# Hybrid encoder layer with grouped experts: one word per block from the table, rows turned before the product, lists in two parts, addition ahead of gather

## What is computed

```
def _moe(h, router_w, router_bias, w_gate, w_up, w_down):
    expert, gates = _route(hf, router_w, router_bias)      # 32 experts, two per token
    ...
    def expert_block(args):
        xb, e = args
        return (jax.nn.silu(xb @ w_gate[e]) * (xb @ w_up[e])) @ w_down[e]
    ...
    out = jnp.zeros((t, d), h.dtype).at[buf_tok].add(
        yb.reshape(rows, d) * buf_g[:, None].astype(h.dtype))

x = _layer_norm(ALPHA * x + (1.0 + g2) * y, ln_ffn_g[l], ln_ffn_b[l])
```

## Time and profile before

| | us |
|---|---|
| median of 3 runs | 1923.19 |
| lowest, highest | 1918.34, 1924.17 |
| the profiled execution | 1921.33 |
| its span, first to last instruction | 1919.5 |
| up to the first block's matmuls | 893.95 |
| blocks, until x1 is read again | 893.95 to 1866.26 |
| reading, last norm, store | 1866.26 to the end |

### The profile page before, as it was taken

One profiled execution on the slowest core, in us unless ns is written; L12 is line 12 of the kernel. 1 busy time (PEld: TensorE's weight loads), 2 busy tenths in 40 slices (PEclk: granted clock), 3 DMA queues, 4 the chain that ended last, 5 costly groups with the idle time before them and its releaser, 6 DMA issues. The chain is left out here.

```text
span 1919.5 us, 55830 instructions
## 1 busy us (share of the span) xinstructions
PE 1541.8 (80%) x17568; PEld 999.4 (52%) x17569; DVE 1015.9 (53%) x2033; ACT 712.8 (37%) x1398; POOL 548.3 (29%) x704
## 2 busy tenths in 40 slices
PE   3999879985899999943887888878888887888840
PEld 2777558863676666632444444444444444444420
DVE  5578778973578888872333332333333334333328
ACT  2313462236576666512323221232222234331217
POOL 0000010000001111122444444444544544544443
PEclk9999889996899999966999999999999999999975
DMA  7657674229433333258879753788567699873247
GB/s 300 220 198 268 204 251 143 88 66 341 167 111 111 120 112 113 97 206 298 320 233 353 248 172 70 272 308 293 172 191 244 220 373 400 282 265 87 38 93 319
DMA packets 130625, 401.51 MB, mean 209 GB/s; under 512 B 15183, under 2 KB 69839, under 8 KB 101760
## 3 DMA queue, kind: packets, MB, share of 16 engines
q1 hardware_dynamic: 95936, 343.85, 47.4%
q0 software_dynamic: 33616, 55.63, 13.3%
q10 hardware_dynamic: 1008, 1.22, 0.2%
HBM read 327.71 MB, written 75.04 MB: 210 GB/s over the span
## 5 line engine op out<-in xcount | busy, mean ns | idle before, releaser
L2034 PE MATMUL psum_gate_up<-gate_up_now,xT 128*32 128x256 f32 x9088 | 535.9, 389 | 172.6 <-DVE xT L2244 169.0
L2034 PEld LDWEIGHTS psum_gate_up<-gate_up_now,xT 128*32 128x32 f32 x9088 | 297.0, 112 | 411.2 <-issue 165.9
L1974 POOL DMA_INDIRECT x_kept<-y_rows,add_index x144 | 230.9, 1603 | 394.6 <-DVE y_rows L2262 387.7
L2047 PE MATMUL psum_y<-down_now,hT 128*32 128x256 f32 x4544 | 274.0, 381 | 5.2 <-issue 3.2
L2087 ACT ACTIVATE gate_silu<-psum_gate_up 128x128 f32<-128x128 f32 x142 | 39.1, 275 | 479.0 <-PE psum_gate_up L2034 479.0
L2047 PEld LDWEIGHTS psum_y<-down_now,hT 128*32 128x32 f32 x4544 | 150.2, 110 | 107.8 <-issue 20.2
L520 PE MATMUL proj_bank<-x_hi,w_hi 128*128 128x512 f32 x448 | 182.4, 407 | 19.8 <-DVE w_lo L632 8.8
L2250 DVE TENSOR_TENSOR hidden<-gate_silu,psum_gate_up 128x128 f32<-128x128 f32 x142 | 40.4, 285 | 298.2 <-ACT gate_silu L2087 236.8
L1959 POOL DMA_INDIRECT x_rows<-h_kept,row_index x148 | 156.5, 1057 | 116.2 <-POOL row_index L1949 102.4
L521 PE MATMUL proj_bank<-x_lo,w_hi 128*128 128x512 f32 x448 | 177.3, 396 | 0.0
L522 PE MATMUL proj_bank<-x_hi,w_lo 128*128 128x512 f32 x448 | 177.1, 395 | 0.0
(11 more groups left out here) (278 smaller groups left out, 2179.2 us busy)
## 6 DMA issues: line engine op xcount, KB each, us to landing
gate_up_raw<-in_w_gate_up SPq DMA_DIRECT2D x128, 1024.0 KB
down_raw<-in_w_down SPq DMA_DIRECT2D x64, 1024.0 KB
x_raw<-in_ada_w SPq DMA_DIRECT2D x16, 1024.0 KB, 4.8
w_raw<-in_w_in SPq DMA_DIRECT2D x28, 512.0 KB
x_raw<-in_xT SPq DMA_DIRECT2D x16, 512.0 KB, 9.7
q_kept<-q_stage SPq DMA_DIRECT2D x32, 256.0 KB, 2.8
q_tile<-q_kept SPq DMA_DIRECT2D x16, 512.0 KB, 4.2
wo<-w_out_kept SPq DMA_DIRECT2D x8, 1024.0 KB, 13.5
```

Source lines behind the costliest of these rows:

```text
L1974: pool.indirect_dma_start(io["x1_rows"], bass.IndirectOffsetOnAxis(add_index[i][:, 0:1], 0), y_rows[:, i, :], None, compute_op=ALU.add).th ...
L2034: last = mm(quarter_of(GU, q)[:, 0:QUARTER], xT[:, k, :], gu_now[:, k, q * QUARTER:(q + 1) * QUARTER], start=(k == 0), stop=(k == DC - 1))
L2047: last = mm(quarter_of(Y, q)[:, 0:QUARTER], hT[:, c, :], down_now[:, c, q * QUARTER:(q + 1) * QUARTER], start=(c == 0), stop=(c == EC - 1))
```

## The change

- **Table.** Three values a block instead of six. One is a word that packs what was four: whether the next block starts an expert, whether this one does, the gate-and-up slot and the expert. The down slot is the expert's lowest bit. ScalarE and VectorE load the word once per block. PE loads nothing in its loop: its waits count by block, and ScalarE and VectorE raise those counters also in blocks without copies.
- **Rows early.** ScalarE keeps x of block j+1 ahead of the weight copies and silu of block j, VectorE turns it ahead of `hide`.
- **Weights freed.** SyncE waits for one count per expert, raised in the expert's first block, instead of the single copies.
- **Row weight.** The gate of each row is copied by GpSimd to `row_weights`, VectorE reads it there and needs no column.
- **Lists.** The column order is by list position, then expert, so the first 256 columns hold every expert's first eight blocks. They are loaded and prepared first, the other 1792 later. Block 0's x and table come ahead of most of the first weight copies on ScalarE.
- **GpSimd.** Addition of block j first, then the gather of block j+4. The last round has no gathers. ScalarE, not GpSimd, waits for the additions of real blocks and frees the rereading of x1.

```
-TABLE_ROWS = 6
-EXPERT, COLUMN, IS_FIRST, N_ALL, GU_SLOT, DOWN_SLOT = range(TABLE_ROWS)
+TABLE_ROWS = 3
+WORD, COLUMN, N_ALL = range(TABLE_ROWS)
+WORD_MAX = 16 * E - 1
 LIST_COLS = E * SLOTS
+EARLY_COLS = 8 * E
...
-                stt(addr[:, :, :], n_before[:, :, :], float(1 - ROWS * LIST_COLS), row[:, :, :], ALU.mult, ALU.add
+                stt(addr[:, :, :], n_before[:, :, :], float(E - ROWS * LIST_COLS), row[:, :, :], ALU.mult, ALU.add
...
+        def parts_of(word):
+
+
+            next_first, first = word & 1, (word >> 1) & 1
+            return next_first, first, word >> 4, ((word >> 2) & 3).with_bounds(min_val=0, max_val=GU_SLOTS - 1)
...
-            for q in range(QUARTERS):
-                sp.dma_start(quarter_of(lists, q)[:, 1:LIST_COLS, :].rearrange("p a b -> p (a b)"),
-                             io["list_rows"][:, 2:2 * LIST_COLS]).then_inc(lists_landed, 16)
+            for landed, first, last in ((early_landed, 1, EARLY_COLS), (lists_landed, EARLY_COLS, LIST_COLS)):
+                for q in range(QUARTERS):
+                    sp.dma_start(quarter_of(lists, q)[:, first:last, :].rearrange("p a b -> p (a b)"),
+                                 io["list_rows"][:, 2 * first:2 * last]).then_inc(landed, 16)
...
-                        last = PIECE * (piece + 1)
-                        sp.wait_ge(gu_by_act, len(GU_BY_ACT) * (e - GU_SLOTS) + sum(k < last for k in GU_BY_ACT))
-                        sp.wait_ge(gu_by_dve, len(GU_BY_DVE) * (e - GU_SLOTS) + sum(k < last for k in GU_BY_DVE))
+                        sp.wait_ge(gu_freed, e - GU_SLOTS + 1)
...
+                ps.tensor_copy(weights[:, i:i + 1], entry_of(column, 1).bitcast(F32)).then_inc(weights_ready, 1)
...
-            def round_of(turn):
+            def round_of(turn, with_next=True):
                 for i in range(RING):
-                    gather(RING * turn + RING + i, i)
                     add_rows(RING * turn + i, i, turn)
+                    if with_next:
+                        gather(RING * turn + RING + i, i)
...
+            last_round = (blocks(pool, but=RING) + (RING - 1)) // RING
             for i in range(1, RING):
                 gather(i, i)
+            pool.wait_ge(quartered, 1)
             round_of(0)
-            with pool.Fori(1, n_rounds) as turn:
+            with pool.Fori(1, last_round) as turn:
                 round_of(turn)
+            round_of(last_round, with_next=False)
             for i in range(RING):
-                wait_apart(pool, (table_ready, 2), (y_added[i], 16 * n_rounds))
-                wait_apart(pool, (table_ready, 2), (x_gathered[i], 16 * n_rounds + 16))
-            pool.sem_inc(all_added, 1)
...
-            def gate_up(j, e):
+            def gate_up(j):
                 pe.wait_ge(x_turned, j + 1)
                 if not isinstance(j, int) or j > 0:
                     pe.wait_ge(hidden_ready, j)
                 for k in range(DC):
                     if k in GU_BY_ACT:
-                        pe.wait_ge(gu_by_act, len(GU_BY_ACT) * e + (GU_BY_ACT.index(k) + 1))
+                        pe.wait_ge(gu_by_act, len(GU_BY_ACT) * j + (GU_BY_ACT.index(k) + 1))
                     else:
-                        pe.wait_ge(gu_by_dve, len(GU_BY_DVE) * e + (GU_BY_DVE.index(k) + 1))
+                        pe.wait_ge(gu_by_dve, len(GU_BY_DVE) * j + (GU_BY_DVE.index(k) + 1))
...
-                following = table_value(pe, EXPERT, j, 0, E - 1)
-                before = table_value(pe, EXPERT, j - 1, 0, E - 1)
-                gate_up(j, following)
-                down(j - 1, before)
-            down(n - 1, E - 1)
+                gate_up(j)
+                down(j - 1)
+            down(n - 1)
...
-            def next_block(j):
-                next_first = table_value(act, IS_FIRST, j + 1, 0, 1)
-                expert, slot = (table_value(act, EXPERT, j + 1, 0, E - 1),
-                                table_value(act, GU_SLOT, j + 1, 0, GU_SLOTS - 1))
-                with act.If(next_first > 0):
-                    copy_gate_up(expert, slot, j, GU_BY_ACT[:-1])
-                silu(j)
+            def step(j):
+                next_first, first, expert, slot = parts_of(table_value(act, WORD, j, 0, WORD_MAX))
                 keep_x(j + 1)
                 with act.If(next_first > 0):
-                    copy_gate_up(expert, slot, j, GU_BY_ACT[-1:])
+                    copy_gate_up(expert + 1, slot, j, GU_BY_ACT[:-1])
+                silu(j)
+                with act.If(next_first > 0):
+                    copy_gate_up(expert + 1, slot, j, GU_BY_ACT[-1:])
+                with act.Else():
+                    act.sem_inc(gu_by_act, len(GU_BY_ACT))
+                if isinstance(j, int) and j == 0:
+                    act.sem_inc(gu_freed, 1)
+                else:
+                    with act.If(first > 0):
+                        act.sem_inc(gu_freed, 1)
+                        copy_down(expert, expert & 1, j - 1)
...
+            copy_gate_up(0, 0, None, GU_BY_ACT[:2])
+            act.wait_ge(early_landed, 16 * QUARTERS)
+            af(lists[:, 1:EARLY_COLS, 0], lists[:, 1:EARLY_COLS, 0], ACT.Identity, bias=C["quarter"]
+               ).then_inc(early_quartered, 1)
             act.wait_ge(counted, 3)
-            nc.scalar.copy(table[:, 4:6, :], B[2][0:1, :].rearrange("p (a b) -> p a b", a=2)[:, :, 0:NJ]
+            nc.scalar.copy(table[:, COLUMN:N_ALL + 1, :], B[2][0:1, :].rearrange("p (a b) -> p a b", a=2)[:, :, 0:NJ]
                            ).then_inc(table_ready, 1)
-            act.wait_ge(lists_landed, 16 * QUARTERS)
-            af(lists[:, 1:LIST_COLS, 0], lists[:, 1:LIST_COLS, 0], ACT.Identity, bias=C["quarter"]
-               ).then_inc(quartered, 1)
             keep_x(0)
+            copy_gate_up(0, 0, None, GU_BY_ACT[2:])
...
+                act.wait_ge(y_added[i], (n + (RING - 1 - i)) // RING * 16)
+            act.sem_inc(all_added, 1)
...
             def weigh_rows(j):
-                column = table_value(dve, COLUMN, j, 0, LIST_COLS + RING - 1)
                 dve.wait_ge(down_chunk_done, EC * (j + 1))
+                dve.wait_ge(weights_ready, j + 1)
                 dve.wait_ge(y_room, j + 1)
-                stt(in_ring(y_rows, j), Y[:, 0:QUARTER], entry_of(column, 1).bitcast(F32), gain2[:, :],
+                stt(in_ring(y_rows, j), Y[:, 0:QUARTER], weights[:, bass.ds(j % RING, 1)], gain2[:, :],
                     ALU.mult, ALU.mult).then_inc(y_ready, 1)
 
-            def next_block(j):
-                next_first = table_value(dve, IS_FIRST, j + 1, 0, 1)
-                expert, slot = (table_value(dve, EXPERT, j + 1, 0, E - 1),
-                                table_value(dve, GU_SLOT, j + 1, 0, GU_SLOTS - 1))
+            def free_down(e):
+                dve.wait_ge(down_by_act, len(DOWN_BY_ACT) * (e + 1))
+                dve.wait_ge(down_by_dve, len(DOWN_BY_DVE) * (e + 1))
+                dve.sem_inc(down_freed, 1)
+
+            def step(j):
+                next_first, first, expert, slot = parts_of(table_value(dve, WORD, j, 0, WORD_MAX))
                 with dve.If(next_first > 0):
-                    copy_gate_up(expert, slot, j)
+                    copy_gate_up(expert + 1, slot, j)
+                turn_x(j + 1)
                 hide(j)
-                turn_x(j + 1)
+                with dve.If(next_first < 1):
+                    dve.sem_inc(gu_by_dve, len(GU_BY_DVE))
+                if not isinstance(j, int) or j > 0:
+                    with dve.If(first > 0):
+                        copy_down(expert, expert & 1, j - 1)
+                        free_down(expert)
+                turn_hidden(j)
+                if not isinstance(j, int) or j > 0:
+                    weigh_rows(j - 1)
```

More of the change, by code:

```diff
@@ L1502, in place @@
                    places.unsqueeze(3).to_broadcast([P, 2, 2, n_starts]), ALU.is_le).then_inc(pos_steps, pos_n.one())
-                ts(row[:, :, :], experts, float(SLOTS), None, ALU.mult).then_inc(pos_steps, pos_n.one())
                 dve.wait_ge(pos_steps, pos_n.now())
@@ L2274, in _ @@
             copy_gate_up(0, 0, None)
             dve.wait_ge(counted, 3)
-            for i in range(2):
-                last = copy(table[:, 2 * i:2 * i + 2, :],
-                            B[i][0:1, :].rearrange("p (a b) -> p a b", a=2)[:, :, 0:NJ])
-            last.then_inc(table_ready, 1)
+            copy(table[:, WORD, 0:P], B[0][0:1, 0:P])
+            copy(table[:, WORD, P:NJ], B[1][0:1, 0:NJ - P]).then_inc(table_ready, 1)
             turn_x(0)
             copy_down(0, 0, None)
+            free_down(0)
```

117 lines of the change are left out of this document (54 added, 63 removed).

## The result

| | before | after |
|---|---|---|
| median of 4 runs each, us | 1921.68 | **1960.93** |
| lowest, highest | 1918.34, 1924.17 | 1957.61, 1961.89 |
| span of the profiled execution | 1919.5 | 1958.7 |

The changed kernel is slower: ratio 1.020 (95% interval 1.018 to 1.022). The forecast was 1824 us, faster.

A forecast was written before the change was run, and what follows sets the result against it. Ordinary blocks were taken as bound by PE's sequencer, blocks around expert changes by VectorE. 190 - 5 - 98 - 10 = 77, + 9 + 13 = 99 us saved: 1822 profiled, 1824 us as median; range 1765 to 1892.

The forecast's parts named there:

- Part 1: PE's loop: both table loads go, so blocks run at 5.3 us, 740 for the stage, 190 us saved.
- rival C: PE's loop: the jump costs what the loads seemed to (1.1 us), ordinary blocks stay at 6.3; 1901 us, chance 0.08.
- Part 2: GpSimd's order: gathers issued behind the addition start one block later; give back 98 us (28 to 170).
- The gather under load: Gather's time with DMA busy: 5.5 us, between 4.9 (behind one weight piece) and 6.9 (one row); alone 2.3.
- The slack of ordinary blocks: Gather's lead in ordinary blocks: 5.05 us where it was about 12; 6 us given back for late weightings.
- Rival D: Gathers last over about 8.2 us when busy, additions ahead in their queue; at 8.5 slower, 1942 us, chance 0.05.
- Rival A: Gathers in the expert stage are never late (2.3 us each): 1754 us, chance 0.15.
- Rival B: GpSimd becomes the bound, making the row weight too: cycle 5.17, or 5.93 us with a dearer hand-over; 1887, chance 0.12.
- Part 3: Weight loading: raw weights freed only at the expert's first block; give back 10 us (0 to 30).
- Part 4: Start: only 255 list columns awaited, block 0 at about 885.9, 8 us sooner; gain 9 us (5 to 11).
- Part 5: End: dead blocks' gathers and additions go, ScalarE waits for real additions only, 4.2 us; gain 13 us (9 to 14).

The follow-up runs named there:

- the best kernel: Changed kernel with row weight, then gather, ahead of the addition, rings of five blocks instead of four, and raw gate-up weights freed once copied: 1726.33 us, ratio 0.898.

## Why the prediction was wrong, point by point

**Part 1, PE's loop: right.** The pace is 5.18, not 5.3: the jump costs nothing that a row shows, and rival C is out. That is 17 us better than counted. The idle time of 0.88 behind a finished xT is gone.

**Part 2, GpSimd's order: the step that failed**, by two terms and a missing third.

- *The gather under load.* I took 5.5 us, from one piece plus 2.3, against the one row that showed 6.9. It is 7.66 on average and up to 8.64. The row had told it, and the start of a stage was no outlier: in that same trace 68 gathers landed 5.3 to 7.8 us after their start, which no wait showed, since the x copies came 3.7 us or more behind the landings.
- *The slack of ordinary blocks.* With 5.5 against 5.05 I gave ordinary blocks 6 us. With 7.66 they are late too: 117 us. At the changes the number was right (17 busy, I had 20), the price was not: 7.4 us each instead of 4.1, and 1.9 at the quiet ones instead of 0.9. For the quiet ones I had read 2.3 us from when the bytes stopped; until ScalarE's copy starts it is 3.2.
- *What lateness does to PE.* I priced the waits alone. Behind an idle time of 3.36 us the 64 matmuls of 1878.21 took 6.46 instead of 3.64, at a granted clock of 0.54:

```profile
1878.21 6.46 PE L2047 MATMUL psum_gate_up<-gate_up_now,xT 128*32 128x256 f32 x64 [3.36 <-DVE hidden L2264]
```

Over the stage PE is busy 798.10 us at 0.92 for what the best kernel does in 730.32 at 1.00: of the 262 us, 187 are PE's waits and 74 are matmuls slower than 5.18 a block, 68 of them more than there. I had no term for that.

**Sum.** For the stage I had 740 + 113 = 853 us; it is 724 + 262 = 985. The failing terms are 149 of give-back, less 17 of better pace.

**Rival D had the direction, at a chance of 0.05, but not its condition.** It put the turning point at 8.2 us and the time at 8.5 at 1942. The mean stayed below 8.2 and the kernel was slower all the same; D had no term for the slower matmuls (74 us) nor for GpSimd's lag (14 us by its own run). D's reason, that gathers last so long because additions stand ahead of them, was wrong in the main: additions make 1.1 us of the 7.66, and the longer ring gives 0.943 with the addition still ahead. What the order costs is the lead, one block. **Rival A** would not have come out even with quiet gathers: 1840 and, with GpSimd's lag gone, 1790, not 1754. **Rival B** is real but smaller, 5.45 instead of 5.93, hidden in the changed kernel and the next thing to bound it once gathers are in time.

**Part 3** 7.7 for 10, measured on the kernel with the row weight ahead of the gather. **Part 4.** Block 0 starts at 888.45, not 885.9, as its own gather took 8.3 us (879.21 to 887.52); the third block is 7.8 sooner, for 9:

```profile
879.21 1.02 POOL L1962 DMA_INDIRECT x_rows<-h_kept,row_index  x1 [0.27 <-POOL row_index L1952]
...
887.52 0.41 ACT L2102 COPY x_now<-x_rows 128x256 f32<-128x256 f32 x1 [3.55 <-DMA x_rows<-h_kept,row_index]
...
888.45 6.41 PE L2047 MATMUL psum_gate_up<-gate_up_now,xT 128*32 128x256 f32 x64 [4.95 <-DVE xT L2258]
```

**Part 5.** From the down product of block 140 to the first load of x1 it is 1904.27 - 1889.67 = 14.6 for 23.66: 9.1 gained, not 13. The last addition to the load is 4.2 as I had it. The last down product came late, waiting 3.28 for a weighting that itself waited for its row weight, and ran at a low clock:

```profile
1889.67 1.90 PE L2056 MATMUL psum_y<-down_now,hT 128*32 128x256 f32 x32
...
1894.85 3.26 PE L2056 MATMUL psum_y<-down_now,hT 128*32 128x256 f32 x32 [3.28 <-DVE y_rows L2276]
...
1900.10 1.58 POOL L1978 DMA_INDIRECT x_kept<-y_rows,add_index  x1 [2.66 <-DVEq L2315]
...
1904.27 0.82 SPq L1941 DMA_DIRECT2D gate_up_raw<-x_kept  x2
```

## What to carry to other kernels

When a change makes the matmuls' pace faster, the lead of every prefetch shrinks with it; count the lead in microseconds at the new pace, and set against it the longest latency that any row shows under load, not one built up from parts. Either issue the prefetch first in its queue or give it one more slot: here both brought the same (1807.57 and 1810.66 us). Small operands that another engine waits for should not stand behind it. Turning inputs early spends slack: it gained 11 us where the input was there and lost 62 where it was late. And a stall of PE is dearer than its length when it brings the clock down: add a term for it.

## What the runs showed of the hardware

- An indirect gather of 128 rows of 1 KB is usable 2.9 to 3.8 us after GpSimd starts it with the weights quiet, and 7.7 us after (up to 8.6) with 1024 KB pieces streaming at about 390 GB/s. Halving the pieces takes 1.1 us off that, leaving out the additions 1.1 as well. By its semaphore a gather lands 2.7 to 3.2 us after its start in the kernel before where weights are quiet, 5.3 to 7.8 where they stream.
- A stall of PE often slows the matmuls behind it. Nine gate-up products of the changed kernel followed 3.0 to 3.6 us without matmuls: six of them took 5.18 to 6.46 us instead of 3.64, three took 3.66 at a granted clock of 1.00, the one of 1766.45 below after 3.42 us. The product of 6.46 had a granted clock of 0.54 (first view), close to the lower of the two levels (1.2 of 2.4 GHz); those of 5.35 show 0.67 and 0.68, a mixture of both levels. Where the clock falls, a stall costs 1.5 to 2.8 us more than its length. A product of 5.35 of the changed kernel, one of the kernel without weight loads, and the product that kept its clock:

```profile
1108.03:1113.20 5.17, 5.17 (x65) 2.95 (x69) 0.76 (x2) 0.00 (x0) 2.73 (x3) 0.67 1.05 393
```

```profile
1165.85:1171.20 5.35, 5.35 (x68) 3.04 (x72) 0.80 (x2) 0.78 (x2) 2.77 (x3) 0.68 0.29 49
```

```profile
1766.45 3.66 PE L2047 MATMUL psum_gate_up<-gate_up_now,xT 128*32 128x256 f32 x64 [3.42 <-DVE hidden L2264]
```

- The loop's jump on PE's queue costs nothing visible: 5.18 us from block to block (1169.93 to 1175.11) is 96 matmuls without idle time of PE.
